# Two-layer hybrid decoder trunk: conditioning matmuls dealt among the first 32 filler items, four filler weight places in layer 0, other DMA costs for the planner

## The reference, cut to what matters

```
for l in range(2):
    mod = silu(c) @ w_ada[l] + b_ada[l]             # "conditioning", 3*2048 columns
    shift, scale, gate = split(mod, 3)
    h = rmsnorm(x, g_pre[l]) * (1 + scale) + shift
    proj = h @ w_in[l]                              # 10368 columns
    u_a, z_a, shifted, gate_a, gate_b = split(proj)
    y_a = (causal_pool(u_a) @ w_pool[l]) * pool_scale[l] * silu(z_a)
    r, k, v, z_b, w_lo, a_lo = split(token_shift(shifted, mu_shift[l]))
    o = wkv7(r, decay(w_lo), k', v', -kk, kk * a)   # state recurrence, 16 heads of 64
    y_b = (groupnorm(o) + bonus) * silu(z_b)
    merged = sigmoid(gate_a) * (y_a @ w_br_a[l]) + sigmoid(gate_b) * (y_b @ w_br_b[l])
    x = x + gate * rmsnorm(merged @ w_out[l], g_post[l])
```

## Time and profile before

| | us |
|---|---|
| median of 3 runs | 5159.62 (5111.48 to 5221.91) |
| profiled execution | 5108.12 |
| its span, slowest core | 5106.6 |
| spans of the 8 cores | 5056.2 to 5106.6 |
| PE busy in the span | 4029.8 (79%) |
| DVE busy | 2670.0 (52%) |
| ACT busy | 1576.6 (31%) |
| mean granted TensorE clock, 8 cores | 0.916 to 0.922 |

### The profile page before, as it was taken

The page is one execution under the profiler, slowest core; times in us unless marked ns, Lnnn a source line. Parts: engine busy times, 40 slices in busy tenths (PEclk is TensorE's granted clock), DMA queues, the critical chain, the costliest instruction groups (busy, mean ns, idle before and its releaser), DMA issues.

```text
span 5106.6 us, 100622 instructions; the slowest of 8 cores (5056.2 to 5106.6 us)
## 1 busy us (share of the span) xinstructions
PE 4029.8 (79%) x37524; PEld 1963.2 (38%) x37524; DVE 2670.0 (52%) x6207; ACT 1576.6 (31%) x3172; POOL 755.5 (15%) x1025
## 2 busy tenths in 40 slices
PE   1159998998998976666748888589988889888688
PEld 1124444444444432333323333244444444444333
DVE  1347777777777730000005556367667776672054
ACT  0234444443443410000000033245444444442101
POOL 1011001011001023333320000210111011102210
PEclk9999999999998987888879999799989899999899
DMA  9432123122123047777785723431323133316993
GB/s 162 103 40 29 23 36 38 21 34 34 22 28 37 20 56 80 87 85 84 85 128 126 143 100 116 79 39 27 38 35 43 19 39 44 45 22 77 132 162 139
DMA packets 634334, 339.03 MB, mean 66 GB/s; under 512 B 491616, under 2 KB 616832, under 8 KB 625408
## 3 DMA queue, kind: packets, MB, share of 16 engines
q0 software_dynamic: 532752, 170.85, 32.5%
q1 hardware_dynamic: 101104, 161.74, 9.9%
HBM read 431.96 MB, written 71.32 MB: 99 GB/s over the span
## 4 chain that ended last, share of the span: by engine, by line
PE 57%; DVE 14%; issue 9%; DMA 9%; ACT 5%; POOL 2%; SPq 2%; DVEq 1%; ACTq 0%; POOLq 0%
PE pb L396 40%; PE pBU L396 7%; DVE big L425 6%; ACT big L409 5%; PE pF L396 5%; DVE big L413 4%; DMA big<-w_in 4%; PE pBY L396 2%; PE pFC L396 2%; DMA big<-w_ada 2%; POOL big L141 2%; DMA big<-sgT 2%; SPq L141 2%; PE pFC L400 1%; DVE big L417 1%
## 5 line engine op out<-in xcount | busy, mean ns | idle before, releaser
L396 PE MATMUL pb<-big 128*128 128x512 bf16 (+4 forms) x10656 | 2686.9, 391 | 479.9 <-DMA big<-w_in 330.8
L396 PEld LDWEIGHTS pb<-big 128*128 128x128 bf16 (+3 forms) x10656 | 952.4, 101 | 1574.8 <-issue 729.7
L141 POOL DMA_DIRECT2D big<-w_in x648 | 482.3, 771 | 2973.8 <-PE pb L396 2186.9
L409 ACT ACTIVATE big<-pb 128x512 f32<-128x512 f32 (+1 forms) x456 | 220.6, 486 | 1506.3 <-PE pb L396 1427.7
L396 PE MATMUL pF<-big 64*64 64x64 bf16 (+2 forms) x11240 | 584.0, 225 | 90.5 <-DVE big L413 67.1
L421 DVE TENSOR_SCALAR big<-big 128x512 bf16<-128x512 f32 (+3 forms) x352 | 134.9, 383 | 840.0 <-ACT big L409 830.5
L413 DVE TENSOR_TENSOR big<-big 128x512 bf16<-128x512 f32 (+8 forms) x800 | 462.6, 580 | 77.9 <-ACT big L409 35.0
L396 PEld LDWEIGHTS pF<-big 64*64 64x64 bf16 (+1 forms) x11240 | 350.3, 109 | 336.7 <-issue 215.0
L409 ACT ACTIVATE big<-pFC 128x512 bf16<-128x512 f32 (+1 forms) x655 | 389.3, 594 | 260.8 <-PE pFC L396 201.2
L396 PE MATMUL pBU<-big 64*64 64x64 bf16 (+2 forms) x2560 | 362.0, 220 | 128.5 <-DVE big L425 63.5
L409 ACT ACTIVATE big<-big 128x512 bf16<-128x512 f32 (+4 forms) x472 | 321.2, 692 | 391.9 <-DVE big L413 193.6
(11 more groups left out here) (118 smaller groups left out, 2558.1 us busy)
## 6 DMA issues: line engine op xcount, KB each, us to landing
big<-w_in POOLq DMA_DIRECT2D x648, 128.0 KB, 4.7
big<-x SPq DMA_DIRECT2D x32, 1024.0 KB, 6.9
big<-w_ada POOLq DMA_DIRECT2D x256, 128.0 KB, 5.6
sgT<-big SPq DMA_DIRECT2D x192, 128.0 KB, 2.1
big<-sgT SPq DMA_DIRECT2D x192, 128.0 KB, 4.1
big<-w_ada POOLq DMA_DIRECT2D x32, 512.0 KB, 36.2
big<-w_out POOLq DMA_DIRECT2D x32, 512.0 KB, 26.5
xmid<-big SPq DMA_DIRECT2D x16, 1024.0 KB, 4.7
```

The costliest lines, as they stand in the source:

```text
L141: return e.dma_start(out=out, in_=in_)
L396: self.P.op("pe", lambda e: e.matmul(rv(out), lhsT, rhs, start=start, stop=stop), r, w, cost=max(140.0, self._n(out) * mult) / 2400.0)
L409: return e.activation(out=rv(out), in_=rv(in_), func=func, scale=scale, **kw)
```

## The change

It alters four things. The planner's cost of a DMA goes from 2.0 to 10.0 us for those from POOL and to 4.0 for the others, and the time for which it holds POOL from 0.06 to 0.8 us. Layer 0 gets four filler weight places, layer 1 keeps three. The items a are dealt two behind each of the first 32 of the 48 other items (u and z first), no longer behind the gates. Stream B gets a `need` for the end of stream E of its block ahead of the three last steps of its norm.

```
@@ dma
-            self._defer.append(("dma", eng, (out, in_, semname), tuple(reads), tuple(writes), 2.0))
+            self._defer.append(("dma", eng, (out, in_, semname), tuple(reads), tuple(writes), 10.0 if eng == "pool" else 4.0))
@@ merge_streams
-            eng_free[eng] = t + (0.06 if kind == "dma" else cost)
+            eng_free[eng] = t + ((0.8 if eng == "pool" else 0.06) if kind == "dma" else cost)
@@ main_phase
-        NPW, ND = 4, 3
+        NPW, ND = 4, (4 if l == 0 else 3)
@@ sB_, ahead of the last steps of the norm
+                    P.ctl("need", "E%d" % si)
                     k.stt(f_y, f_y, col(l, CLG + p), BU, ALU.mult, ALU.mult, ["f_y", ck, "pbU"], ["f_y"])
@@ the list of filler items
+        base = []
         for g in range(4):
-            ditems += [("u", g, 0), ("u", g, 1), ("z", g, 0), ("z", g, 1)]
-        ad = [(0, j) for j in range(32, 48)] + [(1, j) for j in range(48)] if l == 0 else []
-        for c in range(32):
-            ditems.append(("g", c, 0))
-            for (la, j) in ad[2 * c:2 * c + 2]:
-                ditems.append(("a", la, j))
+            base += [("u", g, 0), ("u", g, 1), ("z", g, 0), ("z", g, 1)]
+        base += [("g", c, 0) for c in range(32)]
+        ad = [("a", 0, j) for j in range(32, 48)] + [("a", 1, j) for j in range(48)] if l == 0 else []
+        for i, it_ in enumerate(base):
+            ditems.append(it_)
+            ditems += ad[2 * i:2 * i + 2]
```

## The result

Median 5549.01 us (5492.81 to 5569.88, 4 runs) against 5135.55 us (5083.90 to 5221.91) for the kernel before on the same chip: 1.0796 times as long, 95% interval 1.0662 to 1.0930. This ratio compares only fast executions, those in which neither die (cores 0 to 3, cores 4 to 7) ran clearly slower than the other (of this kernel three, 5486.06 to 5531.57 us). The direction was right, the size was not: 5280 was forecast, and 5549, like each of those three, lies above the range. The profiled execution spans 5530.0 us on core 6 (5463.8 to 5530.0 over the cores), and the mean granted clock of its cores is 0.842 to 0.850, where it was 0.916 to 0.922. Cores 0 to 3 took 5463.8 to 5481.6 us.

The account below looks back on a forecast made before the run. PE's hole was layer 0's 808 us tail, waiting for gate weights; the new planner costs would drain the blocks. 229 - 195 - 67 + 230 - 27 = +170 on 5108 gave 5278, rounded 5280 us; range 5090 to 5460.

Parts of the forecast that it names:

- The mechanism: Planner: four DMAs of a tile estimated serially (31.6 us of POOL), so projections seem late and chunk chains go ahead alone.
- blocks of layer 0, the fourth block: Layer 0's recurrence: fourth block 77 us, four blocks 223 against 190.4, +229 us over seven head pairs.
- Blocks of layer 1: Layer 1's recurrence, same mechanism: four blocks 197 against 164.3 us, +230 over seven, bounds +120 and +310.
- Third block: Third block of a head pair in layer 0: chain, norm, two projections and F, 63.5 us.
- The 16 plain gates: End of layer 0's tail: 16 gates without conditioning items, 13.9 us each.
- The norm: Input norm and transposes of layer 0: transposes interleaved earlier with conditioning matmuls, -67 us, bounds -75 and -45.
- The tail of layer 0: Filler left after layer 0's last block: 613 us against 808, -195, bounds -233 and -138.
- A mixed group: Layer 0's tail: a gate with conditioning items, bound by 18.1 us of DMA time, taken as 19 us, 19 groups.
- Rival C: Blocks: projection loads stand behind filler loads in POOL's queue, each drained block waits a landing; 5500 us, chance 0.09.
- Rivals A and B: Block holes smaller: A, E and P run under lone chains, 4975 us, 0.12; B, DVE work needed anyway, 5110, 0.24.
- The clock of the plain gates: Layer 0's tail: 216.7 ns a matmul, the 2.4 GHz level, though the skill's 13/16 rule would add 51 us.
- the -27: Layer 1's tail: fewer gates -31, unfilled norm +10, and 5 saved at both pipeline starts.

Follow-up runs that it names:

- e1_costs: The kernel before with only the planner's new DMA costs and the `need`; ratio 1.1035 to the kernel before.
- e2_dealt: The changed kernel with the old DMA costs; dealing, four places and the `need` stay; ratio 0.9648 to the kernel before.
- e3_parallel: The changed kernel, its planner no longer making a DMA wait for the last DMA on the same key; ratio 0.9483 to the kernel before.
- e10_cost5: The changed kernel with POOL's DMA cost at 5.0 us instead of 10.0, serial estimate kept; ratio 0.9989 to the kernel before.
- e5_places4: The kernel before with a fourth filler weight place in layer 0 alone; median 5006.98 us, profiled span 4815.6 us.
- e7_warm: The changed kernel with six extra 128-column matmuls in each of the first six chunks of third and fourth blocks; ratio 1.0906 to the kernel before.

## Why the prediction was right and where it was wrong

**The mechanism** was right: serial estimate, projections believed late, chunk chains alone, drained pipeline in the third and fourth block of a head pair. Only sizes were wrong. e1_costs and e2_dealt show that the costs are the cause, e3_parallel that it is the wait of DMA for DMA in the estimate, e10_cost5 that it goes by its length.

**The term that failed: blocks of layer 0, the fourth block.** The four steps were put at 41, 41, 63.5 and 77 us, and took 45.0, 41.2, 66.5 and 90.1: 20.3 us too little for each head pair, or 142 of the 163 us missing over seven; 13.1 of the 20.3 are the fourth block. (The other 21 us are the baseline: the four steps took 187.4 us before in the mean over these seven head pairs, not 190.4.) The fourth block's step by its phases, cut at the same events of PE in each of the seven head pairs, core 6:

| us | taken | block 7 to 8 | mean of seven |
|---|---|---|---|
| norm | 10 | 13.1 | 10.4 |
| projections and filler in line | 17.9 + 6 | 32.7 | 27.6 |
| F | 21 + 2 | 29.9 | 27.0 |
| next chain, up to its copy | 19.3 + 1 | 23.4 | 25.1 |
| sum | 77 | 99.0 | 90.1 |

The norm was sized well; its 13.1 us in block 7 are an exception. The other three phases were each put 4 to 5 us too short. The clock explains little of it: in block 7's step it was granted at 0.97, 0.89 and 0.93 in these three. I had timed them as if each stood alone or as in the first block; but what was held back during the lone chain has to be done in the next phase, and the next chain has other work between its chunks. The rows of PE between norm and F, three of which stand above, carry 20 + 17 + 49 + 13 + 3 + 15 = 117 matmuls of 128x512 in block 7's step. Between F's rounds stand matmuls of E and filler, and F was slower than I took it by its own DVE and ACT steps; that these matmuls are the reason wasn't tested. The order listing has both counts: I read from it where PE was empty, and too little what stands in line when it is full again.

**Blocks of layer 1** failed likewise: 197 us for four blocks against a measured (5106.72 - 3636.74)/7 = 210.0, so 91 us over seven. Here, too, it is the step behind the lone chain: from a fourth block's copy over the next two blocks to the third's copy it took 142.6 us in the mean, where 62.5 + 32 + 34 = 128.5 was taken; from the third's to the fourth's 72.7, where 72.5 was taken. Most of the remaining 35 us are the first head pair's step from the third to the fourth block (41.8 before, 77.7 after), which the term left out because it began to count behind it.

**What came out**, forecast first. Third block: 63.5 and 66.5. The 16 plain gates took 221.17 us, and 16 x 13.9 = 222 was worked out from the earlier trace rows. The norm -67 and -74.6, at the bound -75.

The tail of layer 0 came near its number, -195 and -204, but in part by luck. A mixed group was taken as bound by 18.1 us of DMA time, 19 us. On core 6 the 18 groups from 2188.5 to 2516.98 took 18.2 us each, the one shown 17.2. Yet DMA time was no such bound: on core 0 the groups took 16.4 us each, most of them only the gate's 13.97 and the items' 0.94 us, and its tail was 549.7 us, which is 224 less than the 773.7 of that core before:

```profile
2146.00:2695.70 549.70, 513.15 (x2852) 241.71 (x2910) 105.28 (x236) 86.69 (x147) 212.20 (x285) 0.97 0.83 102
```

In e5_places4 the DMA share of the tail even was 1.13. Core 6 waited 21.4 us for w_in there and core 0 only 4.5; why is open. Nor are all 35 items counted as gates that: the list has 32 gates, and the first ones of the tail still belong to the pooling mixer, with a wait of 7.8 us for w_pool (core 6) that the sum didn't have.

Rival C falls, though its 5500 is the nearest number of all: PE doesn't wait for weights in the blocks. Rivals A and B fall with it: neither E and P under the lone chains nor DVE's work shortened the holes; they came out longer. e2_dealt, where the drains are away, spans 4905.2 us, below even A's 4975.

**The clock of the plain gates.** 221.17 us for 16 gates is 216.0 ns a matmul with all eight cores at work, the 2.4 GHz level, as in the earlier trace rows. By the rule of the Trainium skill in TensorE: Matmul & The Clock Gate, "Seeing it yourself", this stretch would have been 51 us longer, by an estimate; the trace doesn't agree. But a granted clock of 0.81, which is the rule's 13/16, does occur on core 6 elsewhere. A stretch among the blocks, then the plain gates:

```profile
1756.00:1797.00 41.00, 35.95 (x448) 19.11 (x452) 25.89 (x62) 18.02 (x38) 1.16 (x2) 0.81 0.18 10
...
2517.00:2738.00 221.00, 219.89 (x1003) 100.08 (x1024) 30.62 (x66) 37.61 (x63) 44.30 (x60) 1.00 0.50 74
```

**The range.** Its upper end of 5460 was set just short of rival C's 5500. The bounds of the two block terms, +320 and +310, add up with the rest to 5108 + 320 - 195 - 67 + 310 - 27 = 5449, and both terms passed even their upper bounds (+391.8, +356.0). The bounds shared one error, phases that were timed apart, and so they failed together. Small slips of addition (the parts of the -27 give -26, the lower bound of layer 0's blocks +32 and not +35) change nothing.

## What to carry to other kernels

Where a planner fixes the order from estimated costs, a "more realistic" cost is only as good as the rule it enters: 10 us was about the landing of a tile, but added up over four DMAs of one tile it became 41, and the blocks took 392 and 356 us more; with the rule mended the same number gained 63 and 34. When an order drains a pipeline, price a full cycle (count all matmuls in line up to the next chain, and what F takes in their company), not each phase apart. Change and time the parts one by one: this change held a place worth 276 us in the tail, an earlier norm worth some 75 us, a dealing worth 1% alone and negative beside the place, and a cost rule that took more than all of it.

## What the runs showed of the hardware that was not expected

- A fourth weight place raises the tail's DMA share from 0.72 to 1.13 and its rate from 83 to 131 GB/s, and PE's granted clock from 0.82 to 0.99. The gates and conditioning items then need 511.0 instead of 787.3 us. The stretch in e5_places4:

```profile
1830.00:2341.00 511.00, 495.57 (x3162) 237.79 (x3161) 88.63 (x223) 80.86 (x136) 276.77 (x372) 0.99 1.13 131
```

- In the drained stretch of 639.5 to 704.3 us the clock is 0.61 and PE is busy 39.74 of 64.80 us. The eight 128x512 matmuls right behind the chain took 3.62 us, the 49 of block 8's stretch 11.37 us: 0.45 against 0.23 us each.
- 36 extra small matmuls in the chunk chain of each third and fourth block brought no gain (e7_warm): with PE busy 16.11 instead of 11.61 of 18.96 us, the granted clock of the chain stayed 0.50 and its length the same.
